# Opening of a streaming-encoder block: the order in which the first tile, the channel rows and the meta tokens are turned, and the last store

## The reference

```python
D_MODEL = 2048; SEQ = 256; N_META = 16; EPS = 1e-6
def rmsnorm(x, g):
    y = xf * lax.rsqrt(jnp.mean(xf * xf, axis=-1, keepdims=True) + EPS)
    return (y * g.astype(jnp.float32)).astype(x.dtype)

def hybrid_layer(x, norm_g, w_in, b_f, conv_w, w_att_o, w_conv_o, w_out):
    h = rmsnorm(x, norm_g)
    proj = jnp.einsum('bld,dn->bln', h, w_in)
    ...
    o_att = forgetting_attention(heads(q), heads(k), heads(v), log_f)
    y_att = jnp.einsum('blc,cd->bld', o_att * jax.nn.silu(z_att), w_att_o)
    o_conv = gate_b * short_conv(gate_c * u, conv_w)
    y_conv = jnp.einsum('blc,cd->bld', o_conv * jax.nn.silu(z_conv), w_conv_o)
    merged = jax.nn.sigmoid(m_att) * y_att + jax.nn.sigmoid(m_conv) * y_conv
    return x + jnp.einsum('bld,de->ble', merged, w_out)

# 16 meta tokens are put in front of the 256 frames, one layer runs, then
# hdn = rmsnorm(hdn, final_gain); the 256 frames are returned
```

## Time and profile before

| | us |
|---|---|
| median of three runs | 1215.01 |
| profiled execution, its own time | 1215.36 |
| its span in the trace | 1213.4 |
| PE busy | 1196.0 |
| PE: first product of the projection starts | 15.94 |
| PE: last product starts | 1204.92 |

### The profile page before, as it was taken

One profiled execution on the slowest core, in us unless ns is written; L12 is line 12 of the kernel. 1 busy time (PEld: TensorE's weight loads), 2 busy tenths in 40 slices (PEclk: granted clock), 3 DMA queues, 4 the chain that ended last, 5 costly groups with the idle time before them and its releaser, 6 DMA issues.

```text
span 1213.4 us, 18388 instructions
## 1 busy us (share of the span) xinstructions
PE 1196.0 (99%) x7225; PEld 1068.2 (88%) x7225; DVE 956.8 (79%) x1116; ACT 649.9 (54%) x865; POOL 35.7 (3%) x50
## 2 busy tenths in 40 slices
PE   7999999999999999999999999999999999999997
PEld 7998898898888988889888899999999999888885
DVE  6889988988989989989966546877787778755544
ACT  6666555556656566656555444444544554543532
POOL 1000000000000000000000010111011101000000
PEclk9999999999999999999999999999999999999999
DMA  6798898897898888888677866555655565765663
GB/s 215 217 299 279 268 295 268 272 302 258 272 291 286 269 293 282 271 302 265 196 240 262 269 187 182 149 171 168 208 153 172 152 204 164 224 207 178 214 227 114
DMA packets 181393, 280.40 MB, mean 231 GB/s; under 512 B 9312, under 2 KB 128176, under 8 KB 180912
## 3 DMA queue, kind: packets, MB, share of 16 engines
q1 hardware_dynamic: 172000, 263.78, 68.2%
q10 hardware_dynamic: 9312, 15.49, 4.1%
HBM read 270.83 MB, written 8.41 MB: 230 GB/s over the span
## 4 chain that ended last, share of the span: by engine, by line
PE 89%; DVE 8%; issue 1%; ACT 1%; DMA 0%; POOLq 0%; POOL 0%; SPq 0%; DVEq 0%; ACTq 0%
PE ps L1445 22%; PE ps L1447 22%; PE ps L1446 22%; PE ps L1459 13%; PE ps L1460 7%; DVE w_lo L1025 2%; DVE w_lo L1062 1%; DVE w_lo L1059 1%; DVE quads L1041 1%; DVE quads L1043 1%; DVE quads L1039 1%; DMA x_nat<-in_x 0%; PE ps L1468 0%; PE ps L1439 0%; PE ps L1613 0%
## 5 line engine op out<-in xcount | busy, mean ns | idle before, releaser
L909 DVE TENSOR_TENSOR w_lo<-w_raw,w_hi 128x1024 fp32r<-128x1024 f32 x197 | 239.7, 1235 | 99.1 <-ACT w_hi L603 98.4
L1445 PE MATMUL ps<-h,w_hi 128*128 128x258 f32 (+1 forms) x1024 | 294.2, 287 | 1.6 <-DVE w_lo L1025 0.9
L1446 PE MATMUL ps<-h,w_hi 128*128 128x258 f32 (+1 forms) x1024 | 291.7, 285 | 0.0
L1447 PE MATMUL ps<-h,w_lo 128*128 128x258 f32 (+1 forms) x1024 | 291.5, 285 | 0.0
L1459 PE MATMUL ps<-h,w_hi 128*128 128x512 f32 x768 | 273.3, 398 | 0.3 <-DVE w_lo L1025 0.3
L603 ACT CAST w_hi<-w_raw 128x1024 fp32r<-128x1024 f32 x198 | 203.3, 1049 | 112.6 <-PE ps L1447 65.6
L1460 PE MATMUL ps<-h,w_lo 128*128 128x256 f32 x768 | 215.4, 280 | 0.0
L1445 PEld LDWEIGHTS ps<-h,w_hi 128*128 128x128 f32 x1024 | 193.3, 189 | 5.4 <-issue 1.9
L1446 PEld LDWEIGHTS ps<-h,w_hi 128*128 128x128 f32 x1024 | 193.5, 189 | 1.9
L1447 PEld LDWEIGHTS ps<-h,w_lo 128*128 128x128 f32 x1024 | 193.4, 189 | 0.0
L1459 PEld LDWEIGHTS ps<-h,w_hi 128*128 128x128 f32 x768 | 144.2, 188 | 35.5 <-DVE w_lo L1025 1.0
(11 more groups left out here) (197 smaller groups left out, 1827.5 us busy)
## 6 DMA issues: line engine op xcount, KB each, us to landing
w_raw<-in_w_in SPq DMA_DIRECT2D x226, 512.0 KB, 4.8
quads<-in_w_in SPq DMA_DIRECT2D x144, 512.0 KB, 4.4
w_raw<-in_w_conv_o SPq DMA_DIRECT2D x32, 512.0 KB, 5.6
w_raw<-in_w_att_o SPq DMA_DIRECT2D x32, 512.0 KB, 4.8
w_raw<-in_w_out SPq DMA_DIRECT2D x32, 512.0 KB, 4.7
quads<-in_w_in SPq DMA_DIRECT2D x48, 256.0 KB, 4.7
gates_dram<-stage ACTq DMA_DIRECT2D x24, 256.0 KB, 4.8
gate_nat<-gates_dram ACTq DMA_DIRECT2D x8, 512.0 KB, 4.2
```

The lines of the kernel that those rows point to most:

```text
L909: nc.vector.tensor_tensor(w_lo[:, lo_slot(c), :], w_raw[:, c % RAW, :], w_hi[:, hi_slot(c), :].bitcast(F32), ALU.subtract).then_inc(w_spli ...
L1445: nc.tensor.matmul(dst, a_hi, b_hi, start=start, stop=False, skip_group_check=resumed)
L1446: nc.tensor.matmul(dst, a_hi, b_lo, start=False, stop=False, skip_group_check=resumed)
L1447: return nc.tensor.matmul(dst, a_lo, b_hi, start=False, stop=stop, skip_group_check=resumed)
```

## The change

- PE: tile 0's first four blocks are turned directly behind the sixteen filler turns, then the channel rows, then the first half of meta, then tile 1's four blocks. The eight filler turns in between are gone. The second half of meta is turned within the first projection, behind block k = 1.
- DVE and POOL: meta's `var` and `rstd` come first. `var` of a tile is made in one step behind the second sum of squares (`sum1/D + (sum0/D + eps)`); the part with the first sum is made earlier (`first_half`). The second half of meta is multiplied later, behind `split_meta(0)` and ahead of `split_h(0)`.
- Stores: of tile 1, ACT stores the whole left half (128 x 1024, 512 KB) in one transfer; SP stores only the two right pieces. Tile 0 is stored as before.

```diff
@@ block.sync
-                    for side in (1, 0)[:2 - n]:
+                    for side in (1, 0)[:2 - max(n, t)]:
...
-            sp.wait_ge(stored, 8 * 16)
+            sp.wait_ge(stored, 7 * 16)
@@ block.gpsimd
-            for n, (t, rows) in enumerate(((0, P), (2, META), (1, P))):
+            for n, (t, rows) in enumerate(((2, META), (0, P), (1, P))):
@@ block.scalar
-                    act.dma_start(out[t * P:(t + 1) * P, cols], y[:, t, cols]).then_inc(stored, 16)
+                    last = slice(HALF if t == 0 else 0, UNIT)
+                    act.dma_start(out[t * P:(t + 1) * P, last], y[:, t, last]).then_inc(stored, 16)
@@ block.vector
             def mean_square(t):
                 dve.wait_ge(ss_act, 2 * t + 2)
-                nc.vector.tensor_tensor(sums[:, t:t + 1], sumsq[:, t, 0:1], sumsq[:, t, 1:2], ALU.add
-                                        ).then_inc(ss_dve, 1)
                 dve.wait_ge(ss_dve, t + 2)
-                nc.vector.tensor_scalar(var[:, t:t + 1], sums[:, t:t + 1], 1.0 / D, EPS, ALU.mult,
-                                        ALU.add).then_inc(var_done, 1)
+                nc.vector.scalar_tensor_tensor(out=var[:, t:t + 1], in0=sumsq[:, t, 1:2], scalar=1.0 / D,
+                                               in1=sums[:, t:t + 1], op0=ALU.mult, op1=ALU.add).then_inc(var_done, 1)
+
+            def first_half(t):
+                dve.wait_ge(ss_act, 2 * t + 1)
+                nc.vector.tensor_scalar(sums[:, t:t + 1], sumsq[:, t, 0:1], 1.0 / D, EPS, ALU.mult,
+                                        ALU.add).then_inc(ss_dve, 1)
...
-            mean_square(0)
+            dve.wait_ge(ss_dve, 1)
             nc.vector.tensor_scalar(var[0:META, 2:3], meta_sumsq[:], 1.0 / D, EPS, ALU.mult,
                                     ALU.add).then_inc(var_done, 1)
-            dve.wait_ge(rstd_done, 1)
+            first_half(0)
+            mean_square(0)
+            dve.wait_ge(rstd_done, 2)
             normalise(0, 0)
-            dve.wait_ge(rstd_done, 2)
             normalise_meta(0)
+            first_half(1)
             normalise(0, 1)
             mean_square(1)
-            normalise_meta(1)
...
             split_meta(0)
+            normalise_meta(1)
             split_h(0)
@@ block.tensor
             keep_busy(16)
-            pe.wait_ge(rows_landed, 32)
-            rows = (TAPS + 1) * KT
-            nc.tensor.transpose(ps[:, 0, 0:rows], chan_rows[:], ident[0:rows, 0:rows]).then_inc(chan_t, 1)
-            keep_busy(8)
-            pe.wait_ge(chan_done, 1)
...
             for k in range(AHEAD):
                 turn_half(k, 0)
+            pe.wait_ge(rows_landed, 32)
+            rows = (TAPS + 1) * KT
+            nc.tensor.transpose(ps[:, 0, 0:rows], chan_rows[:], ident[0:rows, 0:rows]).then_inc(chan_t, 1)
             turn_meta(0)
             for k in range(AHEAD):
                 turn_half(k, 1).then_inc(h_turned, 1)
-            turn_meta(1)
+            pe.wait_ge(chan_done, 1)
...
                 def after(k):
                     if k + AHEAD < KT:
                         turn(k + AHEAD)
+                    if k == 1:
+                        turn_meta(1)
```

## The result

The changed kernel takes 1218.02 us (median of 17 runs, 1216.25 to 1219.02) against 1215.09 us of the kernel before in as many runs beside it (1214.17 to 1215.92): ratio 1.0021, 95% interval 1.0014 to 1.0029. It is slower, by 2.9 us between the medians. A second set of 11 runs gave a ratio of 1.0017 (1.0008 to 1.0026). The time lies above the range of 1214.5 to 1217.2 us.

The account below looks back on a forecast made before the run. PE was taken as the bound (busy 1196.0 of 1213.4 us). The terms 0 + 0.08 + 0.47 + 0.17 + 0 gave +0.72 us on the median of 1215.01, forecast as 1215.8 us, range 1214.5 to 1217.2.

Parts of the forecast that it names:

- the rival in which it comes back a stretch later: PE's opening: half clock lasts another 3.4 us, +1.7 us, total +2.4, 1217.4 us; chance 0.13.
- the prediction's own signs of being wrong: First product before 15.6, PEclk 0.50 elsewhere or longer, SP's last wait ending over 0.3 us earlier or later.
- The channel rows behind tile 0: PE's opening: channel rows turned at 11.88 instead of 10.97, delaying ACT; filler's removal then wins only 0.44 us.
- DVE's multiplication ahead of `split_h(0)`: Meta's second half on DVE takes 0.67 us, so the first product starts at 16.02, 0.08 later.
- The narrow turns on PE: Eight turns of meta's second half behind k = 1: 0.8 us of wall time, +0.47 us of work displaced.
- The new wait: DVE's `scale_meta(1)` waits for PE's turn of meta's second half; k = 4 starts 0.17 us later.
- the most that a full clock could give: Rival, clock never falls: DVE sets the pace, k = 4 at 21.1, 1214.9 us or 1214.6; chance 0.12.
- Mean in one step, meta first: DVE and POOL's opening: about 0.2 us off each tile's path, hidden behind ACT's chain; costed at 0.
- Tail: Last stores: neither order nor number of transfers decides; 0, bounds -0.3 and +0.9 us.

Follow-up runs that it names:

- e2: Changed kernel with ten filler turns put behind the turn of tile 1, in PE's idle gap; 1214.95 us, ratio 1.0001 to the kernel before.
- e4: Kernel before with only the last left half stored in one transfer; 1214.90 us, ratio 1.0000.
- e8: Kernel before without the eight filler turns between the channel rows and tile 0; 1214.74 us, ratio 1.0001.
- e10: Kernel before with one-step mean, meta's rstd first and the single last store, PE's old order and all filler kept; 1214.59 us, ratio 1.0002.
- e5: Kernel before with only the second turn of meta moved behind block k = 1; 1214.96 us, ratio 1.0006.
- e1: Changed kernel with the second turn of meta back ahead of the first products; 1215.86 us, ratio 1.0011 to the kernel before.
- e3: Changed kernel with ten filler turns behind tile 1 and meta's second turn behind them, ahead of the products; 1214.97 us, ratio 1.0000 to the kernel before.
- c5a: Changed kernel with channel rows first, narrow turns ahead of products, four filler turns, meta's second half multiplied on POOL; 1215.59 us, ratio 1.0005 to the kernel before.

## Why the prediction was wrong

**The step that failed is the clock.** The prediction took the granted clock of the one profiled execution (3.4 us at the half clock) as given for the changed kernel too, and put 0.13 on the rival in which it comes back a stretch later. In the sum the clock thus stood at 0; the runs showed 5.6 us more of PE's work at the half clock, +2.8 us. Shown is that filling PE's gap alone (e2) undoes the loss: the ratio is 1.0001 within 0.1%, all its 11 runs are at 0.998 or 0.999 and none is over 1215.4 us. The evidence had been in rows 5 and 6: there the clock fell behind a gap of 0.60 us, and the prediction itself put the new gap at 1.7 to 2.7 us and then counted the eight filler turns only as time, 0.44 us gained, not as what they did for the clock. The rival was right in kind (the 0.50 did reach to 23) and too cheap: +1.7 us for one stretch, where the profile has 5.6 us more. It missed that the clock falls ahead of the products, as nothing is left for PE behind 13.0 us, not just at their start. With +2.8 for the clock, no wait of DVE and the other terms as they stood, the sum would have been 1218.4; with the measured start of -0.51 for +0.08 it would have been 1217.8.

The length of the gap alone does not decide. With a gap of 0.60 us the clock fell in the profiles of the kernel before, of e4 and of e8, and held in e10's; it also held over 1.20 us in e5's and 1.60 in e2's. What in an execution decides it no run here isolates.

Of the prediction's own signs of being wrong all three came: the first product before 15.6 (15.43), PEclk at 0.50 for longer, and SP's last wait ending, counted from the last product, 0.33 us earlier. Some of its figures were off, with no part in the miss: 1215.01 + 0.72 is 1215.7 and not 1215.8; the forecast with the upper bounds of tail and narrow turns gives 1216.8, and comes near the 1217.2 of the range only with that of DVE's wait too; and PE does pause between the first product and the tail, for 0.3 and 0.9 us, but alike before and after.

The page's rule that the prediction weighed there, the Trainium skill, TensorE: Matmul & The Clock Gate, "Why this matters for your kernels", that only long gaps cost the clock, is again not what the rows show: it fell within the 2.44 us gap, as it had behind 0.60. The same page's Part 1 says that where the clock changes differs from run to run of one kernel, and that the effect on a kernel is under 1%; the two kinds of runs agree with both, 2 us of 1216.

**The channel rows behind tile 0**: forecast `chan` at 12.28 and the first product at 16.02, with PE at the half clock until 13. In e2, whose first turns ran at the half clock, they came at 12.24 and 16.08 (with x landed 0.11 later than in the rows of before): the chain was right. In the changed kernel's profile the clock was up when tile 0 was turned (four turns in 0.44 us), so they came at 11.60 and 15.43.

**DVE's multiplication ahead of `split_h(0)`**: 0.67 us from start to start, as forecast (14.04, 14.71). It was indeed not hidden. That the first product came before 15.6 is owed to the clock at tile 0 and not to this term.

**The narrow turns on PE**: 0.96 us at the half clock, 0.59 at the full one; forecast 0.8 within bounds of 0.61 and 1.22. In work displaced 0.48 us, forecast 0.47. Whether they also keep the clock down longer in runs where it has fallen is open: e1 against the changed kernel, about 1 us, would fit, but e1 changes the gap too, and the slower runs of e5 show a higher time and no lower mean clock. With the gap filled they set off nothing (e2).

**The new wait**: in the changed kernel DVE waited 1.66 us, but PE at the half clock was later still, so it cost 0, not 0.17. At the full clock DVE's chain does set k = 4 (e2, e3), and the most that a full clock could give was forecast as k = 4 at 21.1; e2 has 21.01.

**Mean in one step, meta first**: 0 forecast, 0 measured (e10). **Tail**: 0 forecast, -0.33 in the trace, its lower bound of -0.3; not to be told in the times (e4).

## What to carry to other kernels

Filler on TensorE is not idle time that happens to be spent: before it is taken out, look at the clock of the stretches behind it, and ask what the engine will do in its place. Its removal has no fixed price: alone it cost nothing that can be told (e8), together with the narrow turns moved away and a longer chain on DVE it left a gap of 2.44 us and cost 2.2 to 2.9 us. And where a stretch at the half clock moves in some executions and not in others, one profile is one draw: the mean clock of every run, read beside its time, shows kinds, if only roughly, the pace of the products in a profile shows what the clock column may not, and a median between two kinds can be the time of neither.

## What the runs showed of the hardware

- x's first tile landed between 7.03 and 7.50 us after the start in the profiles, and what follows moved with it; several of the differences sought here were no larger.
- The narrow turns (16 columns, eight of them) take 0.59 us at 2.4 GHz and 0.96 us at 1.2 GHz, less than twice; the wide ones 0.11 and 0.22 each.
- A multiplication of 16 x 1024 by a scalar per partition took 0.73 us on DVE, 1.13 on ACT and 2.93 on POOL, and on POOL it slowed DVE's 128 x 512 beside it to 1.33 us for 0.49 (c5a).
- What is left open: the profile of a changed-kernel run with a mean clock of 0.997 or 0.999, which none of the profiles caught; what besides the gap decides whether the clock falls; and the 0.4 us that six profiles lost between 42 and 65 us.
